# Handing out the quarters of a stick-breaking attention among the slots of a recurrent scan

## What is computed

```python
# group A: RWKV-7, 8 heads x 64, a recurrence over tokens
S = S * w_t + sa * (kk_t * a_t) + v_t * k_t ;  y_t = S r_t
# group B: stick-breaking attention, 8 heads x 64, strictly causal
z = q.k * scale ;  log_beta = log_sigmoid(z) ;  log_1m = log_beta - z  (masked)
A = exp(log_beta + reverse_cumsum(log_1m) - log_1m)  (masked) ;  o = A @ v
```

## Time and profile before

| | |
|---|---|
| median of 3 runs | 1801.07 us |
| the profiled execution, its own time | 1802.92 us |
| its span, first to last instruction | 1801.0 us |
| PE busy in the span | 93% |
| `stage_mix`, first PE instruction to the first of the next stage | 386.9 to 919.4 us |

### The profile page before, as it was taken

The page is one execution under the profiler, slowest core; times in us unless marked ns, Lnnn a source line. Parts: engine busy times, 40 slices in busy tenths (PEclk is TensorE's granted clock), DMA queues, the critical chain, the costliest instruction groups (busy, mean ns, idle before and its releaser), DMA issues. The chain is left out here.

```text
span 1801.0 us, 36214 instructions
## 1 busy us (share of the span) xinstructions
PE 1671.0 (93%) x14676; PEld 1389.2 (77%) x14676; DVE 825.3 (46%) x1125; ACT 698.6 (39%) x1222; POOL 508.5 (28%) x523
## 2 busy tenths in 40 slices
PE   4999999969999998999983987999999999999998
PEld 4999999957777776777742876888888888888886
DVE  5132432426555556555565443444444444444436
ACT  5253443426566565666571443122212211221112
POOL 6332532404434434344452433111111111111110
PEclk7999999979999999999996998999999999999999
DMA  3235266283202213110022213111111111111104
GB/s 140 109 121 183 97 204 208 93 208 93 65 25 72 53 48 77 26 40 23 23 94 82 93 71 124 64 47 47 47 47 50 54 47 47 47 47 47 48 22 164
DMA packets 79386, 143.84 MB, mean 80 GB/s; under 512 B 15505, under 2 KB 51345, under 8 KB 79265
## 3 DMA queue, kind: packets, MB, share of 16 engines
q1 hardware_dynamic: 75520, 128.26, 23.1%
q10 hardware_dynamic: 3744, 13.85, 1.9%
HBM read 104.51 MB, written 37.57 MB: 79 GB/s over the span
## 5 line engine op out<-in xcount | busy, mean ns | idle before, releaser
L1749 POOL TENSOR_TENSOR ffn_ul<-ffn_relu,ffn_uh 128x512 fp32r<-128x512 f32 x64 | 82.9, 1296 | 576.5 <-ACT ffn_uh L1721 576.5
L1778 DVE TENSOR_TENSOR all_acc<-all_acc,ffn_down 128x512 f32<-128x512 f32 x240 | 161.0, 684 | 122.0 <-PE ffn_down L1825 121.4
L618 PE MATMUL inproj_acc<-xn_xh,inproj_wh 128*128 128x346 f32 (+1 forms) x624 | 207.5, 333 | 8.4 <-DVE inproj_wl L539 8.4
L1817 PE MATMUL ffn_up<-all_mh,ffn_wuh 128*128 128x512 f32 x512 | 200.3, 391 | 11.9 <-DVE ffn_wul L1761 11.9
L618 PE MATMUL inproj_acc<-xn_xh,inproj_wl 128*128 128x346 f32 (+1 forms) x624 | 201.2, 322 | 0.0
L618 PE MATMUL inproj_acc<-xn_xl,inproj_wh 128*128 128x346 f32 (+1 forms) x624 | 201.0, 322 | 0.0
L1817 PE MATMUL ffn_up<-all_ml,ffn_wuh 128*128 128x512 f32 x512 | 200.1, 391 | 0.0
L1817 PE MATMUL ffn_up<-all_mh,ffn_wul 128*128 128x512 f32 x512 | 200.0, 391 | 0.0
L1825 PE MATMUL ffn_down<-ffn_wdh,ffn_uh 128*128 128x512 f32 x512 | 199.8, 390 | 0.0
L1825 PE MATMUL ffn_down<-ffn_wdh,ffn_ul 128*128 128x512 f32 x512 | 199.4, 389 | 0.0
L1825 PE MATMUL ffn_down<-ffn_wdl,ffn_uh 128*128 128x512 f32 x512 | 199.2, 389 | 0.0
(11 more groups left out here) (250 smaller groups left out, 3460.4 us busy)
## 6 DMA issues: line engine op xcount, KB each, us to landing
ffn_raw_u<-in_w_up SPq DMA_DIRECT2D x32, 512.0 KB, 3.5
ffn_raw_d<-in_w_down SPq DMA_DIRECT2D x32, 512.0 KB, 4.3
xn_raw<-in_w_in SPq DMA_DIRECT2D x28, 512.0 KB, 4.5
p_scratch<-inproj_out ACTq DMA_DIRECT2D x26, 520.0 KB, 2.7
chunk_scratch<-inproj_fields SPq DMA_DIRECT2D x4, 2720.0 KB, 9.2
mix_swp<-chunk_scratch SPq DMA_DIRECT2D x68, 128.0 KB, 3.6
inproj_rkv<-p_scratch SPq DMA_DIRECT2D x14, 520.0 KB, 4.5
mix_fld<-chunk_scratch SPq DMA_DIRECT2D x17, 256.0 KB, 3.0
```

The source lines that it names most:

```text
L618: last = pe.matmul(acc[g][:, 0:size], w[s][:, kt, :], xx[:, kt, col:col + size], start=(kt == 0 and j == 0), stop=(kt == KD - 1 and j == 2))
L1749: pool.tensor_tensor(ul[s][:, f, cols], relu[j % 2][:, :], uh[s][:, f, cols].bitcast(F32), ALU.subtract).then_inc(u_low.sem, 1)
L1778: dve.tensor_tensor(part, part, downs[o % 4][:, :], ALU.add).then_inc(added.sem, 1)
L1817: last = pe.matmul(ups[j][:, :], w[f][:, k, :], xx[:, k, cols], start=(k == 0 and jj == 0), stop=(k == KD - 1 and jj == 2))
```

## The change

The even share (`k * quarters // slots`) is replaced by a table of what the scan's steps cost. `FRONT_WORK` and `REAR_WORK` have one number for each slot, `QUARTER_WORK` is what a quarter costs in the same unit. After slot k the sum of scan work and quarters given is to be k/144 of the whole. The number of quarters is still 528, and no instruction, buffer or wait is added or taken away; only the places of the quarters in the lists of PE, ACT and DVE move.

```diff
+FRONT_WORK = (12, 4, 4, 8, 8, 12, 4, 8)
+REAR_WORK = (4, 8, 4, 4, 8, 8, 24, 0)
+QUARTER_WORK = 4.2
...
-            k = given = 0
+            whole = CHUNKS * (sum(FRONT_WORK) + sum(REAR_WORK)) + quarters * QUARTER_WORK
+            k = given = scan = 0
...
-                for _ in range(LAP_SLOTS):
+                for slot in range(LAP_SLOTS):
                     next(ahead, None)
                     next(behind, None)
                     k += 1
-                    due = k * quarters // slots
+                    scan += (FRONT_WORK[slot] if n < CHUNKS else 0) + (REAR_WORK[slot] if n else 0)
+                    due = max(given, int((k * whole / slots - scan) / QUARTER_WORK)) if k < slots else quarters
+                    due = min(due, quarters)
```

## The result

| | before | changed |
|---|---|---|
| median | 1801.06 us (4 runs) | 1813.93 us (4 runs, 1813.64 to 1815.82) |
| ratio | | 1.0075, 95% interval 1.0061 to 1.009 |
| the profiled execution, its own time | 1802.92 us | 1815.82 us |
| its span | 1801.0 us | 1813.8 us |
| the mixing, first PE instruction to the first of the next stage | 386.9 to 919.4 us | 387.6 to 932.8 us |

The mixing is 12.7 us longer in the trace. The other stages have their old lengths within 0.7 us. The changed kernel's lines in the mixing are 6 higher: `tri` and `rest` are L1250 and L1251 (L1252 for narrow ones), the exponent is L1127, the first products of a lap are at L1151.

A forecast was written before the change was run, and what follows sets the result against it. PE was taken to bound the mixing, with 32 us of standstill as the ceiling of any gain. Terms -2.9 + 3.4 - 1.5 + 0 - 0.4 = -1.4 us gave 1799.7 us against the median; range 1790 to 1808 us.

The forecast's parts named there:

- rival B: Mixing stage: runs of five or six quarters without scan work let PE wait for the exponent; +11 us, 1812 us, chance 0.10.
- the 22 that were to be its sign: PE's waits of `rest` for DVE's exponent in the mixing: expected about 15 us; above 22 would mean rival B.
- What bounds the stage: Mixing, 386.9 to 919.4 us: PE bounds it with unchanged work; only its standstill, 32 us of 1801, can be won.
- The first term: PE's `rest` waiting for DVE's exponent after `tri`, counted by place in the slots: -2.9 us.
- the price of 0.22 us for a whole triple outside slot 0: Tri, exponent and `rest` within one slot other than slot 0: 0.22 us each, 26 places for 11, +3.3 us.
- the cut at slot 0 after tri: Laps 10 to 12, exponent behind DVE's five copies: 0.7 us each, half of 1.43 us, +2.1 us.
- the bound that I gave this term: The first term, if runs of five and six quarters behave like slot 0: 26 x 0.7 = +18 us instead of +5.7.
- The second term: Chunk loads, issued after `qm` in slot 5: `nrb` comes 1.55 us sooner and waits for them; +3.4 us.
- the 7.6 of the prediction: First load issue to `nrb`: mean of 9.15 us less 1.55; loads taking more than about 7.6 us would end the laps.
- The third term: The scan's chain, mainly `va` waiting for DVE's `krk` copy (4.0 us before, near 2.7 expected): -1.5 us.
- The fourth term: The stage's ends: 0 for 13 more quarters in lap 0 (bounds -2, +2.5), -0.4 us at the end.
- Rival D: PE's clock falls to its lower level at waits for loads in half of the laps; some +20 us, 1820 us, 1 in 100.

The follow-up runs named there:

- e2_inside: Kernel before with its lap totals kept, but laps 1 to 16 dealt out within each lap as the change does it; 1806.44 us, ratio 1.0029 to before.
- f2: Kernel before with four quarters in every slot (slot 6 none in twelve laps), each slot holding tri, values, z, `rest`; 1816.34 us, ratio 1.0091 to before.
- the sister: Kernel before with four quarters a slot (slot 6 none in twelve laps), each slot holding values, z, `rest`, tri; 1818.03 us, ratio 1.0104 to before.
- h_loads_early: Changed kernel with four of a chunk's six loads issued before the wait for `qm`; 1814.06 us, 1.0071 to the kernel before.
- the experiment with dense ends: Kernel before with z-first slots of four quarters, slot 6 empty in laps 1 to 16, 40 quarters in laps 0 and 17; 1786.07 us, 0.992 to before.
- g_cut_moved: Changed kernel with the first quarter of slot 0 in laps 10 to 12 given one slot earlier; 1810.85 us, ratio 1.0048 to the kernel before.

## Why the prediction was wrong, step by step

I forecast -1.4 us; +12.9 was measured. The side was wrong and the time outside the range; rival B had the right place at +11 us and 1 chance in 10, and the 26.6 us of waits lie above the 22 that were to be its sign.

**What bounds the stage** was right: the work of PE did not change, and its standstill did. PE's idle time in the stage went from 32.3 to 41.2 us, by 8.9 of the 12.7 us. The other 3.8 are PE counted as busy (504.1 in place of 500.2 us), which I can't split between the clock and the modelled ends of matmuls.

**The first term failed, and with it the forecast.** It said -2.9 us; the `rest` waits rose by 9.6 us, read place by place as ahead of the prediction:

| places of the joint | before us | said | after us |
|---|---|---|---|
| whole in slot 0 | 6.1 | -5.1 | 0.2 |
| whole in another slot | 2.4 | +3.3 | 14.9 |
| edge of slot 2 or 5 after tri or values | 7.0 | -3.2 | 0.7 |
| edge of slot 0 after tri | 0 | +2.1 | 6.0 |
| all others | 3.8 | 0 | 7.1 |

Both savings came, and larger than said. The failure is the price of 0.22 us for a whole triple outside slot 0. It was the mean of 11 places, all in slots 1, 4 and 5, and all in slots of four quarters, where a whole triple means that the slot begins with tri. The 26 of the new order cost 0.57 us each. Ten are in slot 2, seven in slot 7 and four in slot 3, where the trace of before had not one; they cost 0.70, 0.65 and 0.47 us. But the slot is not what parts the dear ones from the cheap. Sorted by the quarter with which their slot begins:

| the slot begins with | places | us | each |
|---|---|---|---|
| tri (as all before) | 15 | 2.6 | 0.18 |
| `rest` of another task, then tri | 9 | 10.5 | 1.17 |
| z, `rest`, then tri | 2 | 1.8 | 0.88 |

So the old price held for places of the old kind, and the new kind, which only slots of five or more can hold, cost five times as much. Within slot 2 it is 0.38 us (4 places) against 1.09 (5). The trace of e2_inside has the same split within slot 7: three whole triples in slots that begin with tri at 0.05 us, six in slots that begin with z at 1.00. The rows of six of the nine places tell why: ACT's exp and ln go with the quarter of `rest`; if that quarter stands in the same slot, behind the scan's copies of ACT, the ln comes late, DVE's maximum waits for it, and the exponent stands behind the maximum. That was the case in slot 7 of lap 12 above, and in slot 3 of lap 4, which has no scan copy on DVE at all:

```profile
521.62 0.63 ACT L1012 ACTIVATE mix_w<-mix_w 128x512 f32<-128x512 f32 x1
522.29 0.69 DVE L1120 TENSOR_TENSOR mix_w<-mix_z,mix_w 128x512 f32<-128x512 f32 x1 [1.52 <-ACT mix_w L1012]
522.90 0.41 DVE L1127 TENSOR_TENSOR mix_a<-mix_z,mix_cb 128x256 f32<-128x256 f32 x1
523.37 0.39 PE L1250 MATMUL mix_cb<-mix_wsh,mix_rest_r 128*128 128x256 f32 x1 [1.55 <-DVE mix_a L1127]
```

This is read from traces; no run moves that quarter alone. The sister f2, whose slots all begin with tri, fits it: slot 7 costs 0.06 there. Its slot 2 costs 0.59, so that slot is dear by itself too.

The second wrong price is the cut at slot 0 after tri: I halved the 1.43 us of the earlier trace rows because scan work stands on PE in between. But the same work stands ahead of the exponent on DVE, as copies. It was 2.0 us here and 1.42 in the sister. And the places that I had put at nothing rose by 3.3 us in all. Two kinds among them cost nothing before and 4.5 us now: four cut after z at slot 2 have 2.3, five cut after tri at slot 3 have 2.2.

With 0.7 us for every whole triple, as in the bound that I gave this term and in rival B, the term is +9.6 us, to the tenth what came. That is luck in part. B's cause, long runs without scan work, is half of what the traces show: ten slots of five or six quarters that begin with tri cost 0.23 us each, so the length alone does not do it, and the cuts at slot 0 and the places put at nothing, which B does not name, make up the sum.

**The second term, the loads, was wrong too, and harmless.** Said +3.4, measured +0.1, and 0 by taking the wait away (h_loads_early). The first issue of chunk 8 and its `nrb` are now

```profile
619.12 0.37 SPq L841 DMA_DIRECT2D mix_fld<-chunk_scratch  x1
```
```profile
626.36 0.33 PE L1151 MATMUL mix_bank<-mix_fld 64*64 64x128 f32 x2
```

7.2 us apart instead of 9.4. Over the fifteen laps it is 7.8 us in the mean, near the 7.6 of the prediction, and the slack did shrink to 0.0 to 2.4 us. But the loads themselves took 7.0 us in place of 7.4, and of eleven laps with a slack under 0.9 us only two stood at zero. (The price of 0.52 us a quarter holds, though the split was wrong: the seven quarters of the earlier trace rows are four of slot 6, one of them empty since a last task has no `rest`, and three of slot 7.) I had taken each load's old duration as if it belonged to its lap. The estimate by the Trainium skill's "DMA: Bandwidth & Descriptors", section "Anatomy of one DMA — SWDGE (gpsimd) path", by which this term was nothing, came out nearer, though not for its reason: the last load of chunk 8 still took 3.7 us to land and not 2.3.

**The third term was right.** `krk` waits 3.0 us; said near 2.7.

**The fourth term was low.** Laps 0 and 17 went from 20.3 and 17.7 us to 27.5 and 26.4, 15.9 us for 26 quarters, 0.61 each instead of the 0.52 that they take elsewhere, and the experiment with dense ends prices it at 3 to 6 us. I had put 0, with +2.5 as the bound.

**Rival D.** In the stretch from 419 to 919 us the clock was at its lower level of 1.2 GHz three times for 3.4 us (from 690.2, 778.9 and 884.7 us), and in the kernel before not once. The first of them, with the stretches ahead of it and behind it:

```profile
core 0: us, PE busy (x) PEld busy (x) DVE busy (x) ACT busy (x) POOL busy (x), PEclk, DMA share, GB/s
686.00:690.20 4.20, 0.85 (x12) 0.48 (x16) 3.47 (x8) 0.81 (x2) 1.89 (x2) 1.00 0.49 140
690.20:693.60 3.40, 3.40 (x66) 3.18 (x63) 2.30 (x3) 2.29 (x5) 0.00 (x0) 0.50 0.00 0
693.60:697.00 3.40, 3.40 (x42) 2.46 (x41) 2.42 (x3) 2.57 (x5) 2.14 (x3) 1.00 0.03 7
```

It follows the standstill of 3.5 us. But that standstill alone does not decide it. The two other falls came beside waits of 1.7 and 1.4 us, the kernel before had waits up to 1.6 us and no fall, and in g_cut_moved, where waits of 1.0 and 0.9 us stand in this place, the clock fell at 689.3 us all the same. What decides it stays open. The Trainium skill's "TensorE: Matmul & The Clock Gate", section "HAM oscillation — how this bites in real kernels", warns of that for waits for loads; here the falls stood beside waits for DVE. The cost is small: at half clock 3.4 us lose at most 1.7, three of them 5. The three other executions of the changed kernel had a mean clock of 0.970 and 0.971, as the profile of before had 0.971, against 0.967 in this one, and were only 1.6 to 2.2 us faster than it.

## What to carry to other kernels

When two programs are woven on in-order engines, evening out the work of one engine says nothing on what the others have in their lists at that moment. First find the tightest loop of the thing that is dealt out (here tri on PE, exponent on DVE, `rest` on PE), and let the other program's step fall in a joint of that loop behind the exchange, so that its work on both engines comes after; then even out what is left in steps of that loop. Look at a third engine too: what feeds the loop (here exp and ln on ACT) must not be put in the same run just ahead of it. And a price taken from places is good only for places of the same kind: count which kinds the new order has that the old one lacks, and give those the dearest row that you have.

## What the runs showed of the hardware

DVE's clamp (L1109, SBUF to SBUF) and POOL's subtraction (L918) hold each other up, whichever comes second. The 64 clamps of 128x512 in the changed kernel take 0.43 us in the median when they start outside such a subtraction (42) and 1.01 us when they start inside one (22). Even a clamp of half the width ends 0.15 us behind it:

```profile
458.35 1.29 POOL L918 TENSOR_TENSOR mix_wsl<-mix_w,mix_wsh 128x512 fp32r<-128x512 f32 x1
```
```profile
458.53 1.26 DVE L1109 TENSOR_SCALAR mix_w<-mix_z 128x256 f32<-128x256 f32 x1 [0.51 <-ACT mix_z L992]
```

The other way round, a subtraction of 128x512 that starts while a clamp runs takes up to 1.49 us, 1.28 in the median with no clamp beside it. The exponent, which reads PSUM, takes 0.68 us either way. The Trainium skill's "SBUF — State Buffer", section "SBUF: two separate sides", tells of a port pair that DVE and POOL lock against each other for a whole instruction; the trace agrees. This adds up to some 30 us of DVE's time in both kernels, so the total does not tell them apart. Where it falls may: counted only in DVE's unbroken work right ahead of an exponent that PE waited for, and at most at that wait's length, it is 9.0 us in the changed kernel and 5.2 before. That is an upper estimate, by which up to 4 us of the longer waits can come from here; no run takes POOL's subtraction away.
